# A transformer block pair on one core: norms whose root and reciprocal are taken per token, a final norm folded into the next pre-norm, and the normed x written beside the projection

## The reference, cut to what matters

```
def rmsnorm(x, g):
    y = x * rsqrt(mean(x * x, axis=-1) + 1e-6)
    return y * g

# first block: x is (256 tokens, 1024), five FFNs, two mixers
x = x + 0.5 * m2 * swiglu(rmsnorm(x, g) * (1 + m1) + m0, ...)
u = rmsnorm(x, g) * (1 + m4) + m3          # into a mixer
x = rmsnorm(x, final_g)                    # its last line

# second block, for each of two layers
u = rmsnorm(x, pre_norm[l])
y = mixer(u @ w_in[l]) @ w_out[l]
x = x + rmsnorm(y, post_norm[l])
```

## Time and profile before

| what | us |
|---|---|
| median of 3 runs (lowest, highest) | 2298.45 (2296.09, 2300.96) |
| the profiled execution | 2299.87 |
| its span, first to last instruction | 2298.2 |
| TensorE busy in the span | 2137.4 (93%) |
| VectorE busy | 1469.2 (64%) |
| ScalarE busy | 989.6 (43%) |
| reciprocals of norms (L1731), 13 of them | 22.8 |

### The profile page before, as it was taken

One profiled execution on the slowest core, in us unless ns is written; L12 is line 12 of the kernel. 1 busy time (PEld: TensorE's weight loads), 2 busy tenths in 40 slices (PEclk: granted clock), 3 DMA queues, 4 the chain that ended last, 5 costly groups with the idle time before them and its releaser, 6 DMA issues.

```text
span 2298.2 us, 38375 instructions
## 1 busy us (share of the span) xinstructions
PE 2137.4 (93%) x16231; PEld 2017.5 (88%) x16231; DVE 1469.2 (64%) x1814; ACT 989.6 (43%) x1115; POOL 174.3 (8%) x153
## 2 busy tenths in 40 slices
PE   5999999989979899999999899899998989899887
PEld 4999999977749899999999899899997689899867
DVE  4547777788789957777545644547765444775543
ACT  3433455443325534334334433454445345444532
POOL 1000000000010000000000000003210000321000
PEclk9999999999988799999999999989998799899878
DMA  8678688733223357886655355535344044434401
GB/s 322 244 270 288 213 281 284 273 94 110 74 92 129 111 171 246 289 296 204 214 187 183 99 183 182 165 110 162 115 120 138 1 129 129 147 113 122 135 1 56
DMA packets 270792, 383.84 MB, mean 167 GB/s; under 512 B 8441, under 2 KB 230727, under 8 KB 270679
## 3 DMA queue, kind: packets, MB, share of 16 engines
q1 hardware_dynamic: 246983, 293.59, 39.5%
q0 software_dynamic: 22288, 85.02, 10.3%
q10 hardware_dynamic: 1408, 3.59, 0.4%
HBM read 381.06 MB, written 1.11 MB: 166 GB/s over the span
## 4 chain that ended last, share of the span: by engine, by line
PE 80%; DVE 13%; ACT 4%; issue 2%; DMA 0%; SPq 0%; DVEq 0%; ACTq 0%
PE bank L630 21%; PE bank L631 21%; PE bank L632 21%; PE bank L1057 3%; DVE w_hl L1721 2%; PE bank L643 2%; ACT w_hl L1288 1%; DVE e_long L2060 1%; DVE rstd L1731 1%; DVE e_long L2078 1%; PE bank L671 1%; DVE conv_acc L2009 1%; PE bank L1104 1%; PE bank L656 1%; PE bank L683 1%
## 5 line engine op out<-in xcount | busy, mean ns | idle before, releaser
L1721 DVE TENSOR_TENSOR w_hl<-raw,w_hl 128x2048 fp32r<-128x2048 f32 (+1 forms) x281 | 641.1, 2283 | 438.6 <-ACT w_hl L1288 438.3
L1288 ACT ACTIVATE w_hl<-raw 128x2048 fp32r<-128x2048 f32 (+1 forms) x281 | 531.9, 1893 | 220.8 <-PE bank L632 216.6
L630 PE MATMUL bank<-u_hl,w_hl 128*128 128x256 f32 x2080 | 596.5, 287 | 0.0
L631 PE MATMUL bank<-u_hl,w_hl 128*128 128x256 f32 x2080 | 592.6, 285 | 0.0
L632 PE MATMUL bank<-u_hl,w_hl 128*128 128x256 f32 x2080 | 592.2, 285 | 0.0
L630 PEld LDWEIGHTS bank<-u_hl,w_hl 128*128 128x128 f32 x2080 | 403.3, 194 | 10.1 <-issue 8.4
L631 PEld LDWEIGHTS bank<-u_hl,w_hl 128*128 128x128 f32 x2080 | 403.2, 194 | 0.0
L632 PEld LDWEIGHTS bank<-u_hl,w_hl 128*128 128x128 f32 x2080 | 403.1, 194 | 0.0
L630 PE MATMUL bank<-h_hi,w_hl 128*128 128x256 f32 x800 | 226.0, 282 | 2.3 <-DVE h_lo L1810 2.3
L631 PE MATMUL bank<-h_lo,w_hl 128*128 128x256 f32 x800 | 225.4, 282 | 0.0
L632 PE MATMUL bank<-h_hi,w_hl 128*128 128x256 f32 x800 | 225.2, 281 | 0.0
(11 more groups left out here) (373 smaller groups left out, 4106.7 us busy)
## 6 DMA issues: line engine op xcount, KB each, us to landing
ada<-in_ada_w POOLq DMA_DIRECT2D x72, 1024.0 KB, 6.9
raw<-in_w_in SPq DMA_DIRECT2D x60, 1024.0 KB, 5.2
raw<-in_ffn_w_gate SPq DMA_DIRECT2D x55, 1024.0 KB, 7.2
raw<-in_ffn_w_up SPq DMA_DIRECT2D x55, 1024.0 KB, 5.4
raw<-in_ffn_w_down SPq DMA_DIRECT2D x55, 1024.0 KB, 5.0
raw<-in_ssd_w_in SPq DMA_DIRECT2D x20, 1024.0 KB, 5.3
raw<-in_w_out SPq DMA_DIRECT2D x16, 1024.0 KB, 5.2
raw<-in_ssd_w_out SPq DMA_DIRECT2D x8, 1024.0 KB, 5.1
```

Source lines behind the costliest of these rows:

```text
L630: pe.matmul(out_, wh, xh, start=start, stop=False, skip_group_check=True)
L631: pe.matmul(out_, wh, xl, start=False, stop=False, skip_group_check=True)
L1288: nc.scalar.activation(whi[slot][:, 0:n], raw[slot][:, 0:n], ACT.Copy).then_inc(S["hi_done"], 1)
L1721: ve.tensor_tensor(wlo[slot][:, 0:n], raw[slot][:, 0:n], whi[slot][:, 0:n].bitcast(F32), ALU.subtract)\
```

## The change

Nine norms (all but ctx_f0, lat_f0 and ctx_ssd; final is no norm of its own any more) take their sums by token: the squares are the stationary operand and a single column of ones moves, so that the sum of token t stands in partition t, two columns for 256 tokens. Root and reciprocal work on these two columns; two matmuls with the identity spread the result over all partitions in PSUM, where the scales read it. For pre0 two columns move, ones and the squared final gain: the first gives the root of the final norm, both together that of the pre-norm after the final norm. Its scales start from the x that is not normed, with the product of both gains, and the normed x is written behind them, before the projections' later remainders. TensorE waits for it ahead of the first level of the mixer. The bounds are computed in ffn(0) and ffn(1), with a Silu table load behind each of the two places on ScalarE.

```diff
-NORMS = ["ctx_f0", "lat_f0", "ctx_ssd", "lat_ssd", "lat_f1", "l1_f0", "l1_pool", "l1_f1", "final",
+NORMS = ["ctx_f0", "lat_f0", "ctx_ssd", "lat_ssd", "lat_f1", "l1_f0", "l1_pool", "l1_f1",
-SPLIT_NORMS = [n for n in NORMS if n not in ("final", "post0", "post1")]
+SPLIT_NORMS = [n for n in NORMS if n not in ("post0", "post1")]
-SCALED = [n for n in NORMS if n != "final"]
+BY_TOKEN = {"lat_ssd": 3, "lat_f1": 3, "l1_f0": 3, "l1_pool": 3, "l1_f1": 4, "pre0": 2, "post0": 3,
+            "pre1": 2, "post1": 3}
+NBT = {name: i for i, name in enumerate(BY_TOKEN)}
+SCALED = NORMS
...
+            def norm_by_token(name):
+
+                n, b = N[name], bank[BY_TOKEN[name]]
+                fold = name == "pre0"
+                if fold:
+                    pe.wait_ge(S["fold_cols"], 3)
+                for k in range(KB):
+                    pe.wait_ge(S["squares"], KB * n + k + 1)
+                    for tile in range(TT):
+                        dst = b[:, 2 * tile:2 * tile + 2] if fold else b[:, tile:tile + 1]
+                        m = pe.matmul(dst, scratch[:, k, tile * P:(tile + 1) * P],
+                                      fold_cols[:, k, :] if fold else ones[:, 0:1],
+                                      start=k == 0 and tile == 0, stop=k == KB - 1, skip_group_check=True)
+                m.then_inc(S["stat_done"], 1)
+                pe.wait_ge(S["recip_done"], n + 1)
+                for tile in range(TT):
+                    m = pe.matmul(b[:, T + tile * P:T + (tile + 1) * P],
+                                  rstd[n % 2][:, tile:tile + 1].to_broadcast([P, P]), ident, start=True, stop=True)
+                m.then_inc(S["rstd_spread"], 1)
...
-            norm("lat_ssd")
+            norm_by_token("lat_ssd")
             c0 = G["ssd_in"]
...
-            norm("lat_f1")
+            norm_by_token("lat_f1")
             ffn(2)
-            norm("l1_f0")
+            norm_by_token("l1_f0")
...
-            norm("l1_f1", 4)
+            norm_by_token("l1_f1")
             ffn(4)
-            norm("final")
...
                 if i < 0:
+                    pe.wait_ge(S["x_done"], XD["final"])
                     pe.wait_ge(S["scan_done"], l + 1)
...
             for l in range(DEPTH):
-                norm(f"pre{l}")
+                norm_by_token(f"pre{l}")
+                if l == 0:
+                    pe.wait_ge(S["final_recip"], 1)
+                    for tile in range(TT):
+                        m = pe.matmul(bank[3][:, tile * P:(tile + 1) * P],
+                                      rstd[N["pre0"] % 2][:, 4 + tile:5 + tile].to_broadcast([P, P]), ident,
+                                      start=True, stop=True)
+                    m.then_inc(S["final_spread"], 1)
...
-                norm(f"post{l}")
+                norm_by_token(f"post{l}")
...
             def root(name, bk=3):
                 n = N[name]
                 act.wait_ge(S["stat_done"], n + 1)
-                nc.scalar.activation(rms[n % 2][:, :], bank[bk][:, 0:T], ACT.Sqrt, bias=EPS, scale=1.0 / D)\
+                c = slice(0, TT if name in BY_TOKEN else T)
+                nc.scalar.activation(rms[n % 2][:, c], bank[BY_TOKEN.get(name, bk)][:, c], ACT.Sqrt, bias=EPS, scale=1.0 / D)\
                     .then_inc(S["root_done"], 1)
...
-            ffn(0)
+
+            def bounds_exp():
+                act.wait_ge(S["lb_diff"], 1)
+                nc.scalar.activation(small[:, 48:64], small[:, 48:64], ACT.Exp).then_inc(S["lb_exp"], 1)
+                nc.scalar.activation(root_table[:, :], zero_col[:, :], ACT.Silu)
+
+            ffn(0, bounds_exp)
...
             def ctx_norm():
                 root("ctx_ssd")
                 rounded("ctx_ssd", both_hi[:, 1], shifted(0, 1, 1))
+                nc.scalar.activation(root_table[:, :], zero_col[:, :], ACT.Silu)
             ffn(1, ctx_norm)
...
             squares("l1_f1", x, after("pool"))
-            root("l1_f1", 4)
+            root("l1_f1")
             rounded("l1_f1", u_hi, shifted(1, 2, 0))
             ffn(4)
-            squares("final", x, after("ffn4"))
-            root("final")
...
-            act.wait_ge(S["lb_diff"], 1)
-            nc.scalar.activation(small[:, 48:64], small[:, 48:64], ACT.Exp).then_inc(S["lb_exp"], 1)
             for l in range(DEPTH):
-                squares(f"pre{l}", x, after("final" if l == 0 else "out0"))
-                root(f"pre{l}")
+                squares(f"pre{l}", x, after("ffn4" if l == 0 else "out0"))
+                if l == 0:
+                    r = rms[N["pre0"] % 2]
+                    act.wait_ge(S["fold_sum"], 2)
+                    nc.scalar.activation(r[:, 0:TT], r[:, 12:12 + TT], ACT.Sqrt).then_inc(S["root_done"], 1)
+                    act.wait_ge(S["fold_sum"], 3)
+                    nc.scalar.activation(r[:, 4:4 + TT], r[:, 16:16 + TT], ACT.Sqrt, bias=EPS, scale=1.0 / D)\
+                        .then_inc(S["final_root"], 1)
+                else:
+                    root(f"pre{l}")
                 rounded(f"pre{l}", u_hi, lambda k: zero_col[:, 0:1])
                 c0 = G[f"proj{l}"]
...
             def recip(name):
                 n = N[name]
                 ve.wait_ge(S["root_done"], n + 1)
-                ve.reciprocal(rstd[n % 2][:, :], rms[n % 2][:, :]).then_inc(S["recip_done"], 1)
+                c = slice(0, TT if name in BY_TOKEN else T)
+                ve.reciprocal(rstd[n % 2][:, c], rms[n % 2][:, c]).then_inc(S["recip_done"], 1)
+
+            def spread(name):
+                if name not in BY_TOKEN:
+                    ve.wait_ge(S["recip_done"], N[name] + 1)
+                    return rstd[N[name] % 2][:, :]
+                ve.wait_ge(S["rstd_spread"], NBT[name] + 1)
+                return bank[BY_TOKEN[name]][:, T:2 * T]
...
-                ve.wait_ge(S["recip_done"], N[name] + 1)
+                r = spread(name)
                 for k in range(KB + 1):
                     if k < KB:
-                        ve.scalar_tensor_tensor(scratch[:, k, :], src[:, k, :], scale[:, k:k + 1],
-                                                rstd[N[name] % 2][:, :], ALU.mult, ALU.mult).then_inc(S["scaled"], 1)
+                        ve.scalar_tensor_tensor(scratch[:, k, :], r, scale[:, k:k + 1], src[:, k, :],
+                                                ALU.mult, ALU.mult).then_inc(S["scaled"], 1)
...
             def masks():
                 ve.wait_ge(S["mask_in"], 16)
                 ve.tensor_copy(level_mask[:, :, :], mask_in[:, :, :]).then_inc(S["dve_step"], 1)
                 step()
+                ve.memset(fold_cols[:, :, 0], 1.0).then_inc(S["fold_cols"], 1)
+                ve.tensor_tensor(fold_cols[:, :, 1], col("final_g"), col("final_g"), ALU.mult).then_inc(S["fold_cols"], 1)
+                ve.tensor_tensor(fold_g[:, :], col("final_g"), col("pre")[:, 0:KB], ALU.mult).then_inc(S["fold_cols"], 1)
+                ve.tensor_tensor(lbc[:, 0, :], lg[:, 0, :], lg[:, 1, :], ALU.max).then_inc(S["dve_step"], 1)
+                ve.wait_ge(S["dve_step"], step())
+                ve.tensor_tensor(e2, lg, lbc[:, 0, :].unsqueeze(1).to_broadcast([P, 2, H2]), ALU.subtract)\
+                    .then_inc(S["lb_diff"], 1)
+
+            def bounds():
+                ve.wait_ge(S["lb_exp"], 1)
+                ve.tensor_tensor(lbc[:, 0, :], e2[:, 0, :], e2[:, 1, :], ALU.add).then_inc(S["dve_step"], 1)
...
+                ve.tensor_scalar(lbc[:, 1, :], e2[:, 1, :], -1.0, 1.0, ALU.mult, ALU.add).then_inc(S["dve_step"], 1)
+                step()
+                ve.wait_ge(S["dve_step"], step())
...
                 apply("ctx_ssd", xc, mod_a, shifted(0, 1, 1), both_hi[:, 1], both_lo[:, 1])
+                bounds()
             ffn(1, ctx_norm)
...
             ffn(4)
-            recip("final")
-            ve.wait_ge(S["recip_done"], N["final"] + 1)
-            for k in range(KB):
-                ve.scalar_tensor_tensor(x[:, k, :], x[:, k, :], col("final_g")[:, k:k + 1], rstd[N["final"] % 2][:, :],
-                                        ALU.mult, ALU.mult).then_inc(S["x_done"], 1)
+
+            def folded_recip():
+
+                n = N["pre0"]
+                r, b = rms[n % 2], bank[BY_TOKEN["pre0"]][:, 0:2 * TT].rearrange("p (t s) -> p t s", s=2)
+                ve.wait_ge(S["stat_done"], n + 1)
+                ve.tensor_scalar(r[:, 8:8 + TT], b[:, :, 0], EPS / D, EPS * EPS, ALU.mult, ALU.add)\
+                    .then_inc(S["fold_sum"], 1)
+                ve.wait_ge(S["fold_sum"], 1)
+                ve.scalar_tensor_tensor(r[:, 12:12 + TT], b[:, :, 1], 1.0 / D, r[:, 8:8 + TT], ALU.mult, ALU.add)\
+                    .then_inc(S["fold_sum"], 1)
+                ve.tensor_copy(r[:, 16:16 + TT], b[:, :, 0]).then_inc(S["fold_sum"], 1)
+                recip("pre0")
+                ve.wait_ge(S["final_root"], 1)
+                ve.reciprocal(rstd[n % 2][:, 4:4 + TT], r[:, 4:4 + TT]).then_inc(S["final_recip"], 1)
+
+            def final_x():
+
```

(54 more changed lines are left out.)

23 lines of the change are left out of this document (removed).

## The result

The changed kernel takes 2277.91 us (median of 4 runs, 2276.6 to 2279.4) against 2299.7 us of the kernel before (4 runs, 2296.09 to 2301.98): a ratio of 0.9907, 95% interval 0.9896 to 0.9918, some 21.8 us less where 15.0 were forecast. Run once more beside other kernels, it took 2278.62 us (6 runs), against 2298.71 (17 runs): 0.9915 (0.990 to 0.993), 20.1 us less. The profiled execution took 2278.55 us, its span is 2276.9.

The account below looks back on a forecast made before the run. The chain of waits was 80% TensorE and 13% VectorE, so only TensorE's idle gaps at norms would pay. Terms -3.5 + 1.3 - 14.5 + 1.7 = -15.0 us, from 2298.45 to 2283.5 us; range 2275 to 2291.

Parts of the forecast that it names:

- Fold: Final norm and pre0 from one set of squares: 7.1 us from statistics to first product instead of 21.6, 14.5 less.
- the normed x free: Writing the normed x behind pre0's first scales costs nothing; without cover from VectorE's idle time, 3.3 us.
- Seven norms: The seven by-token norms other than pre0 and pre1 gain 0.5 us net each, 3.5 us in all.
- The chain gain: From end of statistics to first scale, 1.27 or 1.72 us instead of 2.30; 0.8 us gained per norm.
- run longer where the clock falls in them: The clock can fall during one-column statistics, costing 0 to 3.5 us per norm, 0.3 us taken as mean.
- rival (b): New hand-overs and clock falls in the statistics make each of seven norms lose 0.5 us: 2290.5 us, chance 0.15.
- Pre1: Statistics of norm pre1 stay at the low clock, 7.1 us instead of 5.52; net loss 1.3 us.
- Bounds: The bounds' eight VectorE operations in ffn(1) stand on the path with a hand-over: 1.7 us more.
- would grow to 4.4: Sign to look for: TensorE's wait for its sum in ffn(1) near 4.4 us instead of 2.7.
- PSUM as source: Scales reading the spread value from PSUM cost nothing extra: 477 ns from PSUM, 479 from SBUF.
- Rival (a): The clock stays up or is back at the first products after five norms and pre0: 2270.5 us, chance 0.10.

Follow-up runs that it names:

- fold_only: The changed kernel with only pre0 keeping sums by token, the other eight norms wide again: 2283.04 us, 0.9934 of the kernel before.
- bounds_old: The changed kernel with the bounds back between ffn(4) and the norm of pre0, without the two Silu loads: 2289.42 us, 0.9962 of the kernel before.
- token_only: The kernel before with the nine norms by token alone, without fold, moved bounds or early table loads: 2294.8 us, 0.9984 of the kernel before.
- wide_all: wide_moving with pre0 too moving 128 columns per matmul: 2266.13 us, 0.986 of the kernel before; 2265.55 us in a second run.
- wide_moving: The changed kernel with 128 equal columns of ones moving instead of one in eight norms, all but pre0: 2268.86 us, 0.9872 of the kernel before.

## Why the prediction was right, and where it was not

The time lies in the range, and the sum fell short by 5 to 7 us. By its own steps, with the means of the two profiles of each kernel (spans 2295.8 and 2276.1, 19.7 us apart), the stages that the sum speaks of give about 16 of the 19.7 us, and the rest came from stages that it left out:

- **Fold, -14.5:** 14.2 us in both pairs of profiles. Its parts too: 7.01 us from statistics to product for 7.1, the second root, reciprocal and spread ahead of the product, the normed x free.
- **Seven norms, -3.5:** six of them (all but lat_ssd) -2.5 us; lat_ssd's stage is equally long with the wide norm in fold_only. The chain gain was right (first scale at 1.28 us for 1.27), and the statistics do run longer where the clock falls in them: lat_ssd 4.67 us, lat_f1 3.87, over all seven 0.27 and 0.34 us on average in the two profiles, for 0.3. Against fold_only the seven gain 1.8 us only, by one profile of each: the reason of rival (b), new falls, shows (behind l1_f0 the changed kernel has 6.8 us at 0.50, fold_only 3.4), its size doesn't.
- **Pre1, +1.3:** statistics 6.99 us for 7.1. The stage's +1.3 us is a mean of +0.2 and +2.4, so that the exact hit is luck. The reason given was half the story: the wide ones end at VectorE's pace, 5.52 us, once the clock is back in time; where it wasn't (fold_only) they took 6.75.
- **Bounds, +1.7:** this step failed. The remainder behind them is 1.5 us late, as the step says, and TensorE's wait for the FFN's remainder grows from 2.3 to 3.8 us. But the wait that I said would grow to 4.4, the one for the modulation sum, fell from 2.7 to 0.4, and ffn(1) is 0.4 us shorter. The wait in the kernel before, then both waits in bounds_old:

```profile
PE bank L630 <- DVE h_lo L1810: 2.3, 1, 2.3
...
PE bank L635 <- DVE h_lo L1860: 2.3, 1, 2.3
PE bank L696 <- DVE ada_acc L1836: 1.1, 1, 1.1
```

  So the bounds explain the growth of the first wait and only the last 0.7 us of the fall of the second: it is 1.1 us in token_only too, which has no bounds there either, and why it isn't 2.7 in them is open. In the kernel before, the clock fell behind that sum, into matmuls (300.7 to 304.1 us in its second profile, and so it did in bounds_old); in the changed kernel no such stretch follows, only the one around the first wait. In the run that moves the bounds out of wide_all's ffn(1), the 1.5 us do come back.
- **PSUM as source, nothing:** 478 ns for the scales. The 120 cycles that the Trainium skill's page "VectorE: DVE Perf Modes" (section "The TRN2 errata") gives for a source in PSUM, for 58 in SBUF, don't show here: the same scales took 479 ns from SBUF.
- **What no step had:** the start (+2.1), ffn(0) (-1.0), the mixer's stage (-3.0), rest of layer 0 (-2.6), rest of layer 1 (+0.8). All five are in code that the change barely touches, and together they are -3.7 us. That the rests of the layers go by where the clock falls is shown above. The mixer's stage is shorter by 2 us or more, and ffn(0) by 0.2 or more, than in either profile of the kernel before, in all twelve profiles of changed kernels, whichever part was undone; the cause of both, and of the late start, is open.
- **Rival (a)** asked for a clock that stays up, 2270.5. It was refuted for this change by the slow stretch behind l1_f0, and the argument from the earlier trace rows was borne out by wide_moving. What I didn't see is that it could be had by widening the moving operand: wide_all, 2266.

## What to carry to other kernels

Shorten the gap at a norm, but feed TensorE wide moving operands up to the gap: statistics of one column saved nothing in time here, since the 16 matmuls take 3.63 us with one column and 3.73 with 128, and lost the clock. Of two norms of the same tensor, fold the first into the second; then move everything off the queues between, an exponential that waits for VectorE above all. And before believing 5 us of a median, compare kernels by stages in two profiles of each, with the kernel before in the same set of runs.

## What was not expected of the hardware

A reciprocal of 2 columns takes 166 ns, against 1753 at 256. One-column matmuls, back to back, didn't hold the clock, though TensorE's row says busy (3.41 of 3.41 us in the earlier trace rows, then 0.50). The clock's slow stretches land in different places in two runs of one program, and the same stage of unchanged code then takes 147.6 or 153.1 us. And the load of x landed at 15.0 and 15.1 us in the two profiles of the kernel before, and at 15.7 to 16.9 in the twelve of changed kernels; why is open.
